# PEER expert rows 106 to 249 gathered whole instead of in halves, and the last six rows shared by TensorE and VectorE

## The chip, the cores and the metric

One core of a Trainium2 chip runs the whole kernel. The metric is the device time of one execution in microseconds, of the kernel before the median of 3 runs: 1603.6 us (1601.72 to 1604.42). Engines are named as in the profile: PE (TensorE), DVE (VectorE), ACT (ScalarE), POOL (GpSimd), SP (SyncE).

## What is computed

One decoder layer on 256 tokens of width 2048 in float32: a projection, a convolution group and a sparse attention group, an output projection and a layer norm, which give x1; then the PEER experts and a second layer norm. The change lies in the PEER part, which takes from about 430 us to the end:

```python
def peer(x, w_q, sub_keys, u_tab, v_tab):
    xt = x.reshape(n_tok, D)                                  # 256 tokens, D = 2048
    q = (xt @ w_q).reshape(n_tok, PEER_HEADS, 2, PEER_DKEY // 2)
    s = jnp.einsum('nhcd,hckd->nhck', q, sub_keys)
    s1, i1 = lax.top_k(s[:, :, 0], 16); s2, i2 = lax.top_k(s[:, :, 1], 16)
    ...                                                       # the 16 best sums of a head, of 256
    experts = jnp.take_along_axis(cand_i, pos, axis=-1)       # 8 heads x 16 experts of 16384, per token
    gates = jax.nn.softmax(top_s, axis=-1)
    h = jax.nn.gelu(jnp.einsum('td,thed->the', xb, u_tab[experts]))
    return jnp.einsum('the,thed->td', gates * h, v_tab[experts])
# then x = layer_norm(ALPHA * x1 + y, ln2_g, ln2_b)
```

## The kernel before

The 256 tokens are two tiles of 128 (tile 0, tile 1), a token per partition. A *row* s = 0 to 255 is one slot of one tile: tile s // 128, head and rank from s % 128. For a row each token needs its own expert: 2048 floats of U and 2048 of V, which lie side by side in `uv_tab` (16 KB an expert). POOL fetches them with an indirect DMA (`gather`, L512 to L515), 128 pieces, one per partition, into one of seven places of 16 KB a partition (`row[k]`, k = PLACE[s]; six places for the first 36 rows). Experts whose first key is among the 24 most frequent ones are not fetched: their number is set out of bounds, and a dense part (`dense_part`, 24 blocks of U in rows 27 to 104; `v_dense`, 24 blocks of V in rows 166 to 239; each 1 MB by SP's queue) computes them for all tokens.

What a row goes through, in this order on the engines:
- DVE `dot(s)` (L1837 to L1846, in the profile L1845): U times x1, summed, after the landing (`u_in`).
- ACT `gelu(s)` (L1271 to L1302): GELU of the dot (L1275), times the gate (`weight`, L1287 or L1289), then, up to row 247, two scalings of V by it (L1302), once V is in.
- PE `add_turned(s)` (L879 to L888): 16 products that turn V by 128 x 128 blocks and add it in PSUM, four banks a tile. From row 166 on (ADDED) it leaves out the last bank's 4, and DVE's `add_last(s)` (L1848 to L1856) adds that quarter of V in SBUF, behind the next row's dot. It is called the small addition here.
- The end of tile 1 is in token order: after row TOKEN_AT - 1 = 247 ACT copies the four banks out, PE turns them back (`turn_back(1, ...)`, L904 to L918), and rows 248 to 253 are added by PE with a diagonal of weights (`add_row`, L890 to L902, L897), four banks each. Rows 254 and 255 (TAIL = 2) are split: banks 0 and 1 by PE, banks 2 and 3 by DVE in PSUM (L2011, the bank additions), after `wait_ge(y_done, ...)`. Then the layer norm of tile 1.

Rows 0 to 25 are gathered whole, one DMA for U and V. From SPLIT = 26 up to row 253 a row is two gathers of 8 KB pieces: the U half in partition order (`u_id`), the V half with the upper and the lower 64 partitions exchanged (`v_id`), which the weights (two writes of 64 partitions, L1287) and the identity `ident_turned` (its tile is called popular in the profile) undo. POOL's order is U(s), V(s - 1), U(s + 1), ... The U half waits for the dot of the row that had the place before (`dots_done`), the V half for PE's products of that row and, for ADDED rows, its small addition (`place_read`, L517). A whole gather waits for the latter two.

DVE does other work between the dots. Up to row 105, in steps of PACE = 7 rows, it ranks the next head's keys; `gates_out` (L1820) of the head before stands behind the dot of a row with s % 7 = 0 and waits for ACT's exponentials, which ACT makes after its work on row s - 1. In rows 107 to 160 come `chunk_keys`, `chunk_gates` and `chunk_mix` for the dense gates, in rows 243 to 252 statistics, `centre` and `scale` of tile 0's layer norm.

The order on each engine is written out by hand in these loops; semaphores alone tie the engines together.

Of the kernel before, what the change touches and what calls it, by code (L numbers as in the profile page):

```python
# [56 lines left out]
TAIL = 2  # L57
TAIL_BANKS = 2
TOKEN_AT = ALL - 8
# [49 lines left out]
SPLIT_USES = [sum(SPLIT <= r and PLACE[r] == PLACE[s] for r in range(s + 1)) for s in range(ALL)]  # L109
# [3 lines left out]
def layer(nc, xT, x_tok, w_stream, w_kw, w_sub, conv_p, cln, bucket1h, rel_bias,  # L113
          b_out, ln1_col, ln_rows, uv_tab, dense_u, out):
    with ExitStack() as ctx:
# [191 lines left out]
        def weight_of(s):  # L307

            n = s if s < SPLIT else SPLIT + s - (ALL - TAIL)
            return weight[:, n:n + 1]  # L310

        def split(s):

            return SPLIT <= s < ALL - TAIL

# [67 lines left out]
        v_in = [sem(f"v_in{k}") for k in range(TAIL)]  # L383
# [4 lines left out]
        passed = {e: sem(f"passed_{e}") for e in ("pe", "act", "dve", "pool")}  # L388
# [63 lines left out]
        def _(pool):  # L452
# [70 lines left out]
            halves = uv_tab.rearrange("n (a d) -> (n a) d", a=2)  # L523
            def v_half(s):

                k, c = PLACE[s], split_col(s)
                place_read(s)
                gather(row[k][:, D:2 * D], halves, v_id[:, c:c + 1], v_half_in[k])

            for s in range(ALL):  # L530
                k = PLACE[s]
                i, j = ROW_OF[s]
                if s == 0:
                    pool.wait_ge(first_picked, 1)
# [12 lines left out]
                if s == WIDER_AT:  # L547
                    pool.wait_ge(unit_scored, LATER)
                if split(s):
                    c = split_col(s)  # L550
                    pool.wait_ge(dots_done, BEFORE_IT[s] + 1)
                    gather(row[k][:, 0:D], halves, u_id[:, c:c + 1], u_in[k])
                    if s > SPLIT:
                        v_half(s - 1)
                    if s == ALL - TAIL - 1:
                        v_half(s)
                    continue
                if BEFORE_IT[s] >= 0:
                    place_read(s)
                if s < ALL - TAIL:  # L560
                    gather(row[k], uv_tab, eid[:, i * SLOTS + j:i * SLOTS + j + 1], u_in[k])
                else:
                    j = s - (ALL - TAIL)
                    gather(row[k][:, 0:D], halves, last_id[:, 0, j:j + 1], u_in[k])
            for j in range(TAIL):
                gather(row[PLACE[ALL - TAIL + j]][:, D:2 * D], halves, last_id[:, 1, j:j + 1], v_in[j])
# [3 lines left out]
        def _(pe):  # L570
# [333 lines left out]
            def turn_back(i, banks):  # L904

                for n in banks:
# [8 lines left out]
                    if i == 1 and n == 3:  # L915
                        pe.wait_ge(y_last_done, len(ADDED))
                        last = pe.matmul(bank(1, 3), ident_turned[:, :], y_last[:, :], start=False, stop=True, skip_group_check=True)
# [100 lines left out]
            for s in range(ALL - TAIL):  # L1018
# [6 lines left out]
                if 2 <= s < TOKEN_AT:  # L1025
                    add_turned(s)
                elif s >= TOKEN_AT:
                    if s == TOKEN_AT:
                        turn_back(1, range(4))
                    add_row(s)  # L1030
# [20 lines left out]
                if BACK_AT <= s < BACK_AT + 2:  # L1051
                    turn_back(0, range(2 * (s - BACK_AT), 2 * (s - BACK_AT) + 2))
            for j in range(TAIL):
                pe.wait_ge(v_in[j], 16)
                add_row(ALL - TAIL + j, TAIL_BANKS)
# [3 lines left out]
        def _(act):  # L1059
# [6 lines left out]
            def upper(u, k):  # L1066

                act.wait_ge(w_in[k], (u - k) * (16 // RING) + 16)
                if not isinstance(u, int) or u >= RING:

                    act.wait_ge(w_used, u - (RING - 1))
                    if not isinstance(u, int):
                        act.sem_inc(passed["act"], 1)
# [317 lines left out]
        def _(dve):  # L1391
# [456 lines left out]
            def add_last(s):  # L1848

                k, n, c = PLACE[s], ADDED.index(s), split_col(s)  # L1850
                dve.wait_ge(weight_done, s + 1)
                dve.wait_ge(v_half_in[k], v_half_from[k] + 16 * SPLIT_USES[s])
                if n:
                    dve.wait_ge(y_last_done, n)
                dve.scalar_tensor_tensor(out=y_last[:, :], in0=row[k][:, D + 3 * 512:2 * D], scalar=weight_turned[:, c:c + 1],
# [7 lines left out]
            def turn_ids(c, n, ready):  # L1863

                cols, ids = slice(c, c + n), posf[1]
                dve.tensor_scalar(u_id[:, cols], ids[:, 0:n], 2.0, None, ALU.mult)
# [63 lines left out]
            for s in range(ALL - TAIL):  # L1930
# [10 lines left out]
                if t == 0 and 1 <= r - 1 < TI * PH:  # L1941
# [39 lines left out]
                if s == CHOSEN_AT + 2:  # L1981
# [11 lines left out]
                for n in range(4):  # L1993
# [3 lines left out]
                    if s == OUT_AT + 2 + n:  # L1997
                        centre(0, n)
                    if s == OUT_AT + 6 + n:
# [4 lines left out]
            for s in range(ALL - TAIL, ALL):  # L2004
                dot(s)
            dve.wait_ge(y_done, ALL - TAIL)
            for s in range(ALL - TAIL, ALL):
                dve.wait_ge(weight_done, s + 1)
                dve.wait_ge(v_in[s - (ALL - TAIL)], 16)
# [3 lines left out]
                link(last)  # L2013
            for n in range(TAIL_BANKS, 4):
# [76 lines left out]
```

## Time and profile before

| | before |
|---|---|
| median of 3 runs | 1603.6 us |
| profiled execution | 1602.62 us |
| its span | 1600.8 us |
| mean granted clock | 0.962 |

```profile
PE 1456.6 (91%) x10102; PEld 1322.7 (83%) x10102; DVE 1269.8 (79%) x2183; ACT 959.7 (60%) x1638; POOL 811.0 (51%) x521
...
PE   9999999999999989998989988888789889878886
...
DVE  5699999775777698888899989888777667657697
ACT  5433345643355557867787788677576546545582
POOL 0000110100123237766666668888888867646883
PEclk9999999999999999999999999788798999999988
DMA  7575544376599999999999999999999999999996
GB/s 258 177 249 183 199 165 158 133 267 246 201 428 424 427 423 417 416 410 405 379 396 412 407 366 344 322 353 368 352 387 394 417 417 412 414 414 405 398 352 219
```

The first line is the busy time of each engine over the span; the others cut the span into 40 slices of 40 us, a digit being the busy share in tenths. PEclk is the granted TensorE clock in tenths of 2.4 GHz, DMA the mean busy share of the 16 DMA engines, GB/s what they moved. A mean over the span says little, since the stages differ: the PEER part begins at the eleventh slice.

### The profile page before, as it was taken

What the parts mean: (1) busy time and instruction counts of PE and PEld (TensorE: products, weight loads), DVE (VectorE), ACT (ScalarE), POOL (GpSimd) and SP (SyncE); (2) the same over time, 40 slices, a digit from 0 to 9 for tenths busy, and PEclk for the clock granted to TensorE, in tenths of its full rate; (3) what the DMA queues carried; (4) which work ended last, traced back from release to release, by engine and by line L of the source; (5) the groups of instructions that cost most, each with busy time, mean ns of one, the idle gap of its engine ahead of it and who ended that gap; (6) DMA issues with size and microseconds to landing.
All of it is one profiled execution on the core that took longest, in us unless ns stands there. A gap on an engine that the chain in (4) does not pass through costs nothing.

```text
span 1600.8 us, 26707 instructions
## 1 busy us (share of the span) xinstructions
PE 1456.6 (91%) x10102; PEld 1322.7 (83%) x10102; DVE 1269.8 (79%) x2183; ACT 959.7 (60%) x1638; POOL 811.0 (51%) x521
## 2 busy tenths in 40 slices
PE   9999999999999989998989988888789889878886
PEld 8999899978889877877778877888778889878873
DVE  5699999775777698888899989888777667657697
ACT  5433345643355557867787788677576546545582
POOL 0000110100123237766666668888888867646883
PEclk9999999999999999999999999788798999999988
DMA  7575544376599999999999999999999999999996
GB/s 258 177 249 183 199 165 158 133 267 246 201 428 424 427 423 417 416 410 405 379 396 412 407 366 344 322 353 368 352 387 394 417 417 412 414 414 405 398 352 219
DMA packets 93840, 540.81 MB, mean 338 GB/s; under 512 B 28754, under 2 KB 29426, under 8 KB 32498
## 3 DMA queue, kind: packets, MB, share of 16 engines
q0 software_dynamic: 72160, 401.97, 63.6%
q1 hardware_dynamic: 20884, 137.00, 22.5%
q8 instruction: 76, 1.25, 0.3%
q14 instruction: 48, 0.39, 0.1%
q10 hardware_dynamic: 672, 0.21, 0.1%
HBM read 682.45 MB, written 4.19 MB: 429 GB/s over the span
## 4 chain that ended last, share of the span: by engine, by line
DMA 24%; DVE 17%; PE 6%; issue 6%; ACT 5%; POOL 4%; POOLq 0%; DVEq 0%; ACTq 0%
DMA uv_row<-in_uv_tab,turned 24%; DVE uv_row L1845 10%; POOL uv_row L514 4%; PE psum L886 3%; ACT uv_row L1302 3%; PE psum L897 1%; PE psum L1002 1%; ACT L1269 1%; PE psum L989 1%; DVE scratch L1675 0%; DVE first_key L1879 0%; ACT turned L1287 0%; DVE key_of L1759 0%; DVE idx L1681 0%; DVE idx L1674 0%
## 5 line engine op out<-in xcount | busy, mean ns | idle before, releaser
L514 POOL DMA_INDIRECT uv_row<-in_uv_tab,turned x456 | 729.8, 1600 | 273.6 <-issue 121.1
L1845 DVE CUSTOM_DVE_ANT_0 uv_row<-uv_row,x 128x2048 f32<-128x2048 f32 x256 | 586.9, 2293 | 142.2 <-DMA uv_row<-in_uv_tab,turned 106.3
L1302 ACT ACTIVATE uv_row<-uv_row,turned 128x1024 f32<-128x1024 f32 (+1 forms) x444 | 451.1, 1063 | 220.8 <-DMA uv_row<-in_uv_tab,turned 216.5
L886 PE MATMUL psum<-popular,uv_row 128*128 128x128 f32 x3224 | 435.8, 289 | 117.7 <-ACT uv_row L1302 116.8
L886 PEld LDWEIGHTS psum<-popular,uv_row 128*128 128x128 f32 x3224 | 380.2, 148 | 163.6 <-ACT uv_row L1302 155.7
L1002 PE MATMUL psum<-scratch,dense_unit 128*128 128x128 f32 x1536 | 188.7, 280 | 0.0
L577 PE MATMUL psum<-xT_hi,w_hi 128*128 128x256 f32 x640 | 182.9, 286 | 2.2 <-DVE w_lo L1423 2.1
L1002 PEld LDWEIGHTS psum<-scratch,dense_unit 128*128 128x128 f32 x1536 | 182.8, 197 | 0.0
L578 PE MATMUL psum<-xT_lo,w_hi 128*128 128x256 f32 x640 | 181.1, 283 | 0.0
L579 PE MATMUL psum<-xT_hi,w_lo 128*128 128x256 f32 x640 | 181.0, 283 | 0.0
L960 PE MATMUL psum<-x1T,dense_unit 128*128 128x256 f32 x768 | 180.1, 381 | 0.0
L1074 ACT ACTIVATE w_hi<-w_raw 128x2048 fp32r<-128x2048 f32 x62 | 118.8, 1916 | 85.1 <-DMA w_raw<-in_w_stream 85.1
L1423 DVE TENSOR_TENSOR w_lo<-w_raw,w_hi 128x2048 fp32r<-128x2048 f32 x62 | 141.6, 2286 | 28.6 <-ACT w_hi L1074 27.8
L960 PEld LDWEIGHTS psum<-x1T,dense_unit 128*128 128x128 f32 x768 | 141.1, 192 | 16.2
L1287 ACT ACTIVATE turned<-dots,row_gate 64x1 f32<-64x1 f32 x456 | 133.3, 292 | 11.0
L577 PEld LDWEIGHTS psum<-xT_hi,w_hi 128*128 128x128 f32 x640 | 122.7, 192 | 6.0 <-issue 2.8
L578 PEld LDWEIGHTS psum<-xT_lo,w_hi 128*128 128x128 f32 x640 | 122.7, 192 | 0.1
L579 PEld LDWEIGHTS psum<-xT_hi,w_lo 128*128 128x128 f32 x640 | 122.7, 192 | 0.0
L1275 ACT ACTIVATE dots<-dots 128x1 f32<-128x1 f32 x256 | 49.4, 193 | 84.8 <-DVE dots L1845 84.3
L514 POOL DMA_INDIRECT uv_row<-in_uv_tab,eid x26 | 38.7, 1490 | 98.2 <-PE psum L886 81.0
L1495 DVE SCALAR_TENSOR_TENSOR scratch<-glu_sb,conv_sb,scratch 128x256 f32<-128x256 f32 x203 | 82.6, 473 | 0.0
L487 POOL TENSOR_TENSOR scratch<-scratch,convT 128x256 f32<-128x256 f32 x6 | 16.5, 2745 | 130.3 <-DVE convT L1499 130.3
(287 smaller groups left out, 1778.0 us busy)
## 6 DMA issues: line engine op xcount, KB each, us to landing
w_raw<-in_w_stream SPq DMA_DIRECT2D x63, 1024.0 KB, 4.9
dense_unit<-in_dense_u SPq DMA_DIRECT2D x24, 1024.0 KB
dense_unit<-in_uv_tab SPq DMA_DIRECT2D x24, 1024.0 KB
wq_first<-in_w_stream SPq DMA_DIRECT2D x8, 1024.0 KB, 12.1
uv_row<-in_uv_tab,turned POOLq DMA_INDIRECT x456
wq_third<-in_w_stream SPq DMA_DIRECT2D x4, 1024.0 KB
xT_raw<-in_xT SPq DMA_DIRECT2D x4, 512.0 KB, 6.4
turned_rows<-dist_row POOLq DMA_DIRECT2D x1, 2048.0 KB
```

The costliest lines, as they stand in the source:

```text
L514: pool.indirect_dma_start(dst, None, tab, bass.IndirectOffsetOnAxis(ap=ids, axis=0), bounds_check=tab.shape[0] - 1, oob_is_err=False).then ...
L577: pe.matmul(dst, a[0], b[0], start=first, stop=False)
L578: pe.matmul(dst, a[0], b[1], start=False, stop=False)
L579: return pe.matmul(dst, a[1], b[0], start=False, stop=last)
L886: last = pe.matmul(bank(i, b // 4)[:, b % 4 * P:(b % 4 + 1) * P], row[k][:, D + b * P:D + (b + 1) * P], order[:, :], is_transpose=True, st ...
L960: last = pe.matmul(side[v % 2][:, 0:S], w[:, c, :], x1T[:, c, :], start=c == 0, stop=c == KC - 1)
L1002: last = pe.matmul(bank(i, n)[:, b % 4 * P:(b % 4 + 1) * P], dense_unit[v % 2][:, b * P:(b + 1) * P], mixed[:, v, i * P:(i + 1) * P], star ...
L1074: act.activation(w_hi[k], w_raw[k], ACT.Copy).then_inc(hi_done, 1)
L1287: whole = act.activation(weight_turned[to, c:c + 1], dots[of, s:s + 1], ACT.Identity, scale=row_gate[of, i, j:j + 1])
L1302: act.activation(v, v, ACT.Identity, scale=w).then_inc(scaled, 1)
L1423: dve.tensor_tensor(w_lo[k], w_raw[k], w_hi[k].bitcast(F32), ALU.subtract).then_inc(lo_dve, 1)
L1845: dve.tensor_tensor_reduce(row[k][:, 0:D], row[k][:, 0:D], x1[:, ROW_OF[s][0], :], 1.0, 0.0, ALU.mult, ALU.add, dots[:, s:s + 1]).then_inc ...
```

## The change

It does the following.
- Rows 106 to 249 (WHOLE) are gathered whole, one DMA of 16 KB pieces, in partition order. They wait for the place as a whole gather does. Their weight is one write of 128 partitions (L1289), PE turns them with `ident`, and no engine waits for a V half.
- TOKEN_AT goes from 248 to 250 and TAIL from 2 to 6: rows 248 and 249 become turned rows with a small addition, rows 250 to 255 are all shared, banks 0 and 1 by PE and 2 and 3 by DVE. All six are gathered in halves in partition order.
- DVE waits for all of `turn_back` after the dot of 251, and from then on alternates a dot and the two bank additions of the row two before.
- `gates_out` and the marking of head (0, 2) come one row later, `centre` and `scale` of tile 0 are drawn together into rows 245 to 248.
- Smaller: the row numbers in `u_id` are no longer doubled for whole rows (one more 0.17 us instruction in two of the blocks of 16 rows), the y_last product uses `ident`, unused semaphores go.

```diff
@@ -54,9 +54,9 @@
-TAIL = 2
+TAIL = 6
 TAIL_BANKS = 2
-TOKEN_AT = ALL - 8
+TOKEN_AT = ALL - TAIL
@@ -106,7 +106,16 @@
-SPLIT_USES = [sum(SPLIT <= r and PLACE[r] == PLACE[s] for r in range(s + 1)) for s in range(ALL)]
+
+WHOLE = range(IDS_AT + 1, TOKEN_AT)
+
+
+def in_two(s):
+
+    return s >= SPLIT and s not in WHOLE
+
+
+SPLIT_USES = [sum(in_two(r) and PLACE[r] == PLACE[s] for r in range(s + 1)) for s in range(ALL)]
@@ -306,12 +315,18 @@
         def weight_of(s):
 
-            n = s if s < SPLIT else SPLIT + s - (ALL - TAIL)
+            if s in WHOLE:
+                return weight_turned[:, s - SPLIT:s - SPLIT + 1]
+            n = s if s < SPLIT else SPLIT + s - TOKEN_AT
             return weight[:, n:n + 1]
 
         def split(s):
 
-            return SPLIT <= s < ALL - TAIL
+            return in_two(s) and s < TOKEN_AT
+
+        def wait_v_half(engine, s):
+
+            engine.wait_ge(v_half_in[PLACE[s]], v_half_from[PLACE[s]] + 16 * SPLIT_USES[s])
@@ -521,11 +535,16 @@
+            def in_halves(s):
+
+                return split(s) or TOKEN_AT <= s < ALL
+
             def v_half(s):
 
-                k, c = PLACE[s], split_col(s)
+                k = PLACE[s]
                 place_read(s)
-                gather(row[k][:, D:2 * D], halves, v_id[:, c:c + 1], v_half_in[k])
+                j, c = s - TOKEN_AT, split_col(s)
+                gather(row[k][:, D:2 * D], halves, last_id[:, 1, j:j + 1] if j >= 0 else v_id[:, c:c + 1], v_half_in[k])
@@ -550,20 +569,18 @@
                     pool.wait_ge(dots_done, BEFORE_IT[s] + 1)
                     gather(row[k][:, 0:D], halves, u_id[:, c:c + 1], u_in[k])
-                    if s > SPLIT:
-                        v_half(s - 1)
-                    if s == ALL - TAIL - 1:
-                        v_half(s)
-                    continue
-                if BEFORE_IT[s] >= 0:
-                    place_read(s)
-                if s < ALL - TAIL:
-                    gather(row[k], uv_tab, eid[:, i * SLOTS + j:i * SLOTS + j + 1], u_in[k])
+                elif s >= ALL - TAIL:
+                    pool.wait_ge(dots_done, BEFORE_IT[s] + 1)
+                    gather(row[k][:, 0:D], halves, last_id[:, 0, s - TOKEN_AT:s - TOKEN_AT + 1], u_in[k])
                 else:
-                    j = s - (ALL - TAIL)
-                    gather(row[k][:, 0:D], halves, last_id[:, 0, j:j + 1], u_in[k])
-            for j in range(TAIL):
-                gather(row[PLACE[ALL - TAIL + j]][:, D:2 * D], halves, last_id[:, 1, j:j + 1], v_in[j])
+                    if BEFORE_IT[s] >= 0:
+                        place_read(s)
+                    of = eid[:, s:s + 1] if s < SPLIT else u_id[:, s - SPLIT:s - SPLIT + 1]
+                    gather(row[k], uv_tab, of, u_in[k])
+                if in_halves(s) and in_halves(s - 1):
+                    v_half(s - 1)
+                if in_halves(s) and not in_halves(s + 1):
+                    v_half(s)
@@ -1024,10 +1041,6 @@
                 if 2 <= s < TOKEN_AT:
                     add_turned(s)
-                elif s >= TOKEN_AT:
-                    if s == TOKEN_AT:
-                        turn_back(1, range(4))
-                    add_row(s)
@@ -1050,8 +1063,9 @@
+            turn_back(1, range(4))
             for j in range(TAIL):
-                pe.wait_ge(v_in[j], 16)
+                wait_v_half(pe, TOKEN_AT + j)
                 add_row(ALL - TAIL + j, TAIL_BANKS)
@@ -1847,12 +1861,11 @@
             def add_last(s):
 
-                k, n, c = PLACE[s], ADDED.index(s), split_col(s)
+                k, n = PLACE[s], ADDED.index(s)
                 dve.wait_ge(weight_done, s + 1)
-                dve.wait_ge(v_half_in[k], v_half_from[k] + 16 * SPLIT_USES[s])
                 if n:
                     dve.wait_ge(y_last_done, n)
@@ -1938,7 +1954,7 @@
-                if t == 0 and 1 <= r - 1 < TI * PH:
+                if t == 1 and 1 <= r - 1 < TI * PH:
                     gates_out(r - 1)
@@ -1978,7 +1994,7 @@
-                if s == CHOSEN_AT + 2:
+                if s == CHOSEN_AT + 3:
                     mark(0, 2)
                     divide(0, 2)
@@ -1994,23 +2010,31 @@
-                    if s == OUT_AT + 2 + n:
+                    if s == OUT_AT + 2 + n // 2:
                         centre(0, n)
-                    if s == OUT_AT + 6 + n:
+                    if s == OUT_AT + 4 + n // 2:
                         scale(0, n)
@@ -1994,23 +2010,31 @@
-            for s in range(ALL - TAIL, ALL):
-                dot(s)
-            dve.wait_ge(y_done, ALL - TAIL)
-            for s in range(ALL - TAIL, ALL):
+            def add_token(s):
+
                 dve.wait_ge(weight_done, s + 1)
-                dve.wait_ge(v_in[s - (ALL - TAIL)], 16)
+                wait_v_half(dve, s)
                 for n in range(TAIL_BANKS, 4):
                     last = dve.scalar_tensor_tensor(out=bank(1, n), in0=row[PLACE[s]][:, D + n * 512:D + (n + 1) * 512],
                                                     scalar=weight_of(s), in1=bank(1, n), op0=ALU.mult, op1=ALU.add)
                 link(last)
+
+            dot(TOKEN_AT)
+            add_last(TOKEN_AT - 1)
+            dot(TOKEN_AT + 1)
+            dve.wait_ge(back_turned, 4 * TI)
+            for s in range(TOKEN_AT + 2, ALL):
+                dot(s)
+                add_token(s - 2)
+            for s in range(ALL - 2, ALL):
+                add_token(s)
```

## Rows read from the trace of the kernel before

**Rows 1.** Busy by stage: stretch, length, engines, PEclk, DMA share, GB/s.

```profile
440.00:590.00 150.00, 142.62 (x865) 128.27 (x864) 112.26 (x281) 83.34 (x137) 43.52 (x29) 0.98 1.01 426
600.00:760.00 160.00, 144.81 (x920) 127.86 (x919) 137.22 (x327) 120.86 (x206) 108.49 (x73) 0.98 1.01 412
760.00:955.00 195.00, 176.56 (x1143) 156.56 (x1141) 171.99 (x410) 152.40 (x252) 125.92 (x88) 1.00 0.99 393
955.00:998.00 43.00, 35.86 (x299) 32.58 (x298) 40.11 (x40) 37.36 (x67) 36.02 (x17) 1.00 0.93 349
998.00:1177.00 179.00, 152.50 (x1081) 144.79 (x1081) 147.53 (x148) 121.33 (x211) 153.97 (x82) 0.84 0.95 351
1177.00:1235.00 58.00, 54.82 (x363) 45.60 (x364) 38.65 (x37) 42.77 (x82) 48.61 (x31) 0.88 0.99 389
1235.00:1530.00 295.00, 255.36 (x2192) 248.51 (x2191) 200.21 (x202) 162.54 (x332) 209.90 (x138) 0.98 1.01 410
1530.00:1578.00 48.00, 39.41 (x217) 29.11 (x217) 42.88 (x48) 34.07 (x76) 41.07 (x22) 0.89 0.97 348
```

**Rows 2.** Groups of instructions, 998:1177: line, shapes, count, busy and mean, idle and releasers.

```profile
L514 POOL DMA_INDIRECT uv_row<-in_uv_tab,turned x82 | 154.0, 1878 | 25.0 <-issue 22.3 <-PE psum L886 2.7
...
L886 PE MATMUL psum<-popular,uv_row 128*128 128x128 f32 x657 | 104.3, 319 | 26.5 <-ACT uv_row L1302 26.4
```

**Rows 3.** Chain that ended last, 1050:1100 and 1380:1450: start, us, what.

```profile
1054.60 7.71 DMA uv_row<-in_uv_tab,turned
...
1358.17 24.67 DMA uv_row<-in_uv_tab,turned
...
1393.52 31.11 DMA uv_row<-in_uv_tab,turned
...
1424.64 1.60 DVE uv_row L1845
...
1428.11 28.68 DMA uv_row<-in_uv_tab,turned
```

**Rows 4.** Timeline at 1060 us: start, us, instruction, idle before it.

```profile
1059.24 0.99 POOL L514 DMA_INDIRECT uv_row<-in_uv_tab,turned  x1 [0.30 <-issue]
...
1060.45 2.29 DVE L1845 CUSTOM_DVE_ANT_0 uv_row<-uv_row,x 128x2048 f32<-128x2048 f32 x1 [2.52 <-DMA uv_row<-in_uv_tab,turned]
...
1060.54 3.07 POOL L514 DMA_INDIRECT uv_row<-in_uv_tab,turned  x1 [0.30 <-issue]
```

**Rows 5.** Waits of DVE, 760:955: for whom, us in total, times, longest.

```profile
DVE gsum L1825 <- ACT gate L1269: 15.8, 7, 2.6
```

**Rows 6.** Groups of instructions on POOL, 440:590, gathers of whole rows.

```profile
L514 POOL DMA_INDIRECT uv_row<-in_uv_tab,eid x22 | 34.7, 1576 | 93.7 <-PE psum L886 81.0 <-DVE x L1635 8.6 <-issue 4.0
```

**Rows 7.** Timeline of DVE, 984:1006, two dots three rows apart.

```profile
984.02 2.28 DVE L1845 CUSTOM_DVE_ANT_0 uv_row<-uv_row,x 128x2048 f32<-128x2048 f32 x1
...
994.83 2.28 DVE L1845 CUSTOM_DVE_ANT_0 uv_row<-uv_row,x 128x2048 f32<-128x2048 f32 x1
```

**Rows 8.** Groups of instructions on DVE, 1235:1530, the small addition.

```profile
L1855 DVE SCALAR_TENSOR_TENSOR y_last<-uv_row,turned,y_last 128x512 f32<-128x512 f32 x67 | 50.2, 749 | 20.2 <-issue 20.2
```

**Rows 9.** Timeline of the end, 1540 to 1590 us.

```profile
1540.74 2.29 DVE L1845 CUSTOM_DVE_ANT_0 uv_row<-uv_row,x 128x2048 f32<-128x2048 f32 x1
...
1552.70 2.29 DVE L1845 CUSTOM_DVE_ANT_0 uv_row<-uv_row,x 128x2048 f32<-128x2048 f32 x1
...
1563.73 1.02 PE L917 MATMUL psum<-y_last,popular 128*128 128x512 f32 x2
...
1578.16 2.29 DVE L1845 CUSTOM_DVE_ANT_0 uv_row<-uv_row,x 128x2048 f32<-128x2048 f32 x1 [4.14 <-DMA uv_row<-in_uv_tab,last_id]
...
1581.43 2.29 DVE L1845 CUSTOM_DVE_ANT_0 uv_row<-uv_row,x 128x2048 f32<-128x2048 f32 x1 [0.97 <-DMA uv_row<-in_uv_tab,last_id]
...
1585.39 2.86 DVE L2011 SCALAR_TENSOR_TENSOR psum<-uv_row,weight,psum 128x512 f32<-128x512 f32 x4 [1.66 <-PE psum L897]
```

More of the change, by code:

```diff
@@ L382, in layer @@
         u_in = [sem(f"u_in{k}") for k in range(PLACES + 1)]
-        v_in = [sem(f"v_in{k}") for k in range(TAIL)]
         dots_done, gelu_done, scaled, y_done = (sem(n) for n in ("dots_done", "gelu_done", "scaled", "y_done"))
@@ L387, in layer @@
         total_step, conv_summed, sq_step, sq_summed = (sem(n) for n in ("total_step", "conv_summed", "sq_step", "sq_summed"))
-        passed = {e: sem(f"passed_{e}") for e in ("pe", "act", "dve", "pool")}
+        act_passed = sem("act_passed")
         block = ctx.enter_context(nc.Block())
@@ L916, in turn_back @@
                         pe.wait_ge(y_last_done, len(ADDED))
-                        last = pe.matmul(bank(1, 3), ident_turned[:, :], y_last[:, :], start=False, stop=True, skip_group_check=True)
+                        last = pe.matmul(bank(1, 3), ident[:, :], y_last[:, :], start=False, stop=True, skip_group_check=True)
                     last.then_inc(back_turned, 1)
@@ L1072, in upper @@
                     if not isinstance(u, int):
-                        act.sem_inc(passed["act"], 1)
+                        act.sem_inc(act_passed, 1)
                 act.activation(w_hi[k], w_raw[k], ACT.Copy).then_inc(hi_done, 1)
@@ L1848, in add_last @@
             def add_last(s):
-                k, n, c = PLACE[s], ADDED.index(s), split_col(s)
+                k, n = PLACE[s], ADDED.index(s)
                 dve.wait_ge(weight_done, s + 1)
-                dve.wait_ge(v_half_in[k], v_half_from[k] + 16 * SPLIT_USES[s])
                 if n:
                     dve.wait_ge(y_last_done, n)
-                dve.scalar_tensor_tensor(out=y_last[:, :], in0=row[k][:, D + 3 * 512:2 * D], scalar=weight_turned[:, c:c + 1],
+                dve.scalar_tensor_tensor(out=y_last[:, :], in0=row[k][:, D + 3 * 512:2 * D], scalar=weight_of(s),
                                          in1=y_last[:, :], op0=ALU.mult, op1=ALU.add).then_inc(y_last_done, 1)
@@ L1865, in turn_ids @@
                 cols, ids = slice(c, c + n), posf[1]
-                dve.tensor_scalar(u_id[:, cols], ids[:, 0:n], 2.0, None, ALU.mult)
+                for a, b, of in ((c, WHOLE[0] - SPLIT, 2.0), (WHOLE[0] - SPLIT, WHOLE[-1] + 1 - SPLIT, 1.0), (WHOLE[-1] + 1 - SPLIT, c + n, 2.0)):
+                    a, b = max(a, c), min(b, c + n)
+                    if a < b:
+                        dve.tensor_scalar(u_id[:, a:b], ids[:, a - c:b - c], of, None, ALU.mult)
                 dve.tensor_scalar(v_id[HALF:P, cols], ids[0:HALF, 0:n], 2.0, 1.0, ALU.mult, ALU.add)
```

## The prediction

> **What bounds the kernel now.** The unit is a row: one slot s of the 256, that is one gather of a U row and a V row per token, one dot (L1845), one weighted addition. I first read the busy time by stage, with granted clock, share of the DMA engines and GB/s [rows 1], the stages cut at the dots counted in order: 600 to 955 us are rows 29 to 105, 955 to 998 rows 107 to 117, 998 to 1177 rows 118 to 159, 1177 to 1235 rows 160 to 173, 1235 to 1530 rows 174 to 241, then the end. The change touches rows 106 to 255.
>
> In 600:760, 760:955 and 1235:1530 the DMA share is 0.99 to 1.01 at 393 to 412 GB/s: the transfers bind, or nearly do. Between them, 998:1177 moves 351 GB/s. There POOL is busy 154.0 us and stands idle 25.0 us before its gathers, in pieces that are the issue of the next one, 0.3 us each [rows 2]. The sum is the whole 179: POOL never waits for a place, it is the bound. The same sum gives 48.61 + 31 x 0.3 = 57.9 of 58 us in 1177:1235, and 41.07 + 22 x 0.3 = 47.7 of 48 in 1530:1578 [rows 1]. The chain of waits says the same from the other side: a gather in it takes 7.71 us from issue to landing at 1055 us, and 31.11 us at 1393 us [rows 3]. In the one place the queue is short of work, in the other it is as full as the ring of seven places lets it be.
>
> Why a gather costs POOL 1878 ns on average [rows 2]: one takes 0.99 us, the next, issued while a dot runs, takes 3.07 us and ends at 1063.61, 0.87 us after that dot [rows 4]. Two a row cost 2 x (1.88 + 0.30) = 4.36 us, and 179 us for 41 rows (82 gathers) is 4.37.
>
> **The change, part by part. (A) gates_out one row later (t = 0 to t = 1), through row 106.** DVE waits 15.8 us in 760:955 for the exponentials, 7 times, 2.3 us each [rows 5]. One row later a dot of 2.29 us stands between and the result is there. Next in line is the DMA: the stage carries 195 x 393 = 76.6 MB, which at the 412 GB/s of the stage before takes 186 us [rows 1]. So at most 9 us, at least 0; the earlier waits of this kind lie in stages that the DMA binds and are worth nothing. I take 6. Marking (0, 2) a row later costs nothing: its identifiers are first used at row 32.
>
> **(B) One gather for two, rows 106 to 249, where POOL binds (998 to 1235, 237 us).** POOL falls to at most 3.07 + 0.3 = 3.4 us a row. If a gather of 16 KB pieces took twice as long, 2 + 0.87 + 0.3 = 3.2 us would still fit. Whole gathers exist now, in rows 0 to 25, with a mean of 1576 ns against 1878 [rows 6], so I expect no more than that. Next: DVE needs 994.83 - 984.02 = 10.81 us for three rows while it makes the chunk keys, 3.60 a row [rows 7]; 42 rows are 151 us, a gain of at most 28. And the DMA: 351 x 179 + 389 x 58 = 85.4 MB, which is 200 us at the 426 GB/s of 440:590 (where rows are whole), 208 at 410, 213.5 at 400, 217 at 393 [rows 1]. I take 400 (reason under C): a gain of 23.5 us. Ends: 33 (151 us, and 53 for the last fourteen rows) and 10 (over half of it kept by other waits).
>
> Beside this stand ACT, which loses one of two weight writes and its wait for the V half, and PE. PE is 152.5 us busy of 179 at a mean clock of 0.84, and idle for ACT's scaled rows in the rest (26.4 us) [rows 1, 2]. In 955:998 rows went at DVE's pace with PE busy 35.86 of 43 and the clock at 2.4 GHz throughout [rows 1]. So I cost PE at nothing; what it costs without that cover is the second rival.
>
> **(C) The same where the DMA binds (1235 to 1530, 295 us, 410 GB/s, 121 MB).** For: rows that are whole move at 426 GB/s, halves at 412 and 410 [rows 1]; 121 MB would then take 284 us, 11 less. Against: a half of a place is given back early now. The U half that lands at 1424.62 is read by its dot, and the next U gather of the place is issued at 1428.11, 3.5 us later; flights are 24.67 to 31.11 us [rows 3]. A whole place comes back only when its V has been read too, last by the small addition of DVE, which stands behind the dot of the next row, and that dot waits for the next landing. A period is 295 us for 69 rows (138 gathers), 4.3 us, so this is 4.3 + 2.3 + 0.75 [rows 8] = 7.4 us, with POOL's own wait some 8. Of a place's round of 7 x 4.3 = 30 us, about 22 are then in flight. A shorter queue evens out less between the 16 engines, whose shares of kept experts differ from row to row. The nearest rows are 351 GB/s with 7.7 us in flight and 410 with 25 to 31. I take 400, between the 393 and the 410 of the busy stages: 302.5 us, a loss of 7.5. Ends: a gain of 11, and a loss of 18 (386 GB/s).
>
> The Trainium skill (HBM Reference, "Specifications (TRN2)") says that a core streaming alone reaches about 425 GB/s, bounded by its 16 DMA engines. By that figure B and C together would take 206.4 / 0.425 = 486 us, 46 less than now. The stage 440:590 agrees (426); the stages of rows with left-out experts do not reach it (412, 393, 410), and the sum goes by them.
>
> **(D) The end, from the dot of row 244 (1540.74) to the last bank addition (1588.25).** Moving the centre and scale steps of tile 0 forward changes no sum. Added on DVE: two small additions (rows 248, 249) of 0.75 us, and eight bank additions (twelve for four) of 2.86 / 4 = 0.72: 7.2 us. Gone: its waits for the last two landings, 4.14 and 0.97, and for PE, 1.66 [rows 8, 9]. The landings are late because POOL issues back to back there, which one gather a row up to 249 ends; PE is late because it multiplies 28 banks, and 12 remain. A new wait: after the dot of 251 DVE stands at back_turned (all four banks), with four dots and twelve additions queued behind it. Now the last row ahead of that turn, 247, has its dot over at 1554.99 and the turn over at 1564.75, 9.8 us [rows 9]. DVE fills 2 x 2.29 + 2 x 0.75 = 6.1 of them, 3.7 is wait. Sum: 7.2 - 6.8 + 3.7 = +4.1. Ends: 0 (the turn is sooner, since ACT has a weight less to write) and +8 (a landing is late after all).
>
> Sum: -6 - 23.5 + 7.5 + 4.1 = -17.9. The profiled execution has 1602.6 us (span 1600.8 and 1.8 around it), so 1584.7; the median of the runs is 1.0 above it, 1585.7. I write 1585.
>
> **Rivals. (1) The queue stays full with 22 us in flight.** Whole rows move at 418 GB/s in C (289.5 us), B ends at DVE's pace. A -9, B -33, C -5.5, D +2: -45, 1558. For: 426 GB/s in 440:590. Against: in those rows no expert is left out, in the later ones the engines' loads are uneven.
>
> **(2) PE keeps what POOL gives.** If the clock stays at a mean of 0.84 in 998:1177 and half of PE's 26.4 us of idle stays between ACT's scaling and its products, that stage needs 152.5 + 13 = 165.5 us and B is worth 13.5: -6 - 13.5 + 7.5 + 4.1 = -8, 1595. For: PE is busy 85% there. Against: 955:998 at full clock, with rows at 3.6 us.
>
> **(3) Slower: the ring starves the DMA.** A whole place returns only when its V has been read, and some engines run dry while others hold the row up. B and C carry 206.4 MB in 532 us. With A and D (-6 + 4) the change breaks even at 534 us, a mean rate of 386 GB/s; below that it loses. At 369, halfway from 386 to the 351 of the short queue, it is 559 us: +25, 1627. For: 348 to 351 GB/s in every stage where little is in flight [rows 1]. Against: 22 us is nearer to the full queue than to 7.7.
>
> The Trainium skill (DMA: Bandwidth & Descriptors, "The descriptor swizzle") has it that a 128-partition transfer gives each engine a fixed set of 8 partitions, and partitions 64 apart go to different engines. The halves, whose V side is swapped by 64, then spread a token's load over two engines, and whole rows put it on one. That speaks for this rival and against the change; no row here shows a single engine.
>
> **How the numbers follow.** Forecast 0.62 (own range 1575 to 1597), rival 1 0.14, rival 2 0.14, rival 3 0.10. The range, 1563 to 1600, leaves out rival 3 and the better half of rival 1. A measurement tells about 0.2% (3.2 us) from no change: faster 0.85, within 0.06, slower 0.09.
>
> **What would show it.** A: no DVE wait for the gates, and the dot of row 106 some 6 us earlier. B: POOL idle for PE or for places and not for issue between rows 118 and 159, some 3.8 us a row, about 400 GB/s. C: the rows of this stage at 4.4 us each, flights near 22 us; 410 GB/s or more speaks for rival 1, under 386 for rival 3. D: a DVE wait of 3 to 4 us ahead of the dot of 252, none for the last landings. What would make it wrong: whole rows outside 393 to 410 GB/s, or a whole gather that holds POOL longer than a half does.

## The result and the profile after

The median of 22 runs is 1605.8 us, against 1600.1 us for 22 runs of the kernel before on the same chips: a ratio of 1.0038, 95% interval 1.0026 to 1.0050. The change makes the kernel slower by 0.4%. The prediction said 1585 and gave 0.09 to slower. The profiled execution has 1606.4 us, its span 1604.5 (before 1602.6 and 1600.8).

The page of after, in the order of the lines shown of before: busy time over the span, then slices of 40 us.

```profile
PE 1446.6 (90%) x10094; PEld 1321.9 (82%) x10094; DVE 1274.6 (79%) x2195; ACT 929.8 (58%) x1492; POOL 568.6 (35%) x377
...
PEclk9999999999999999999999998897899999999978
DMA  7565544376599999999999999999999999999993
GB/s 258 180 243 182 198 168 158 132 299 225 225 426 426 425 422 416 417 411 408 380 403 416 405 365 380 366 420 382 354 381 421 405 349 407 418 388 365 359 364 133
```

POOL has 144 gathers less and is busy 568.6 us in place of 811.0. In the six slices from 960 us on the rate is 354 to 420 GB/s where it was 322 to 387, but in the three from 1400 us on it is 359 to 388 where it was 398 to 414. By stage, the cuts at the same dots as in [rows 1] (rows 106, 118, 160, 174, 241), in its columns:

```profile
600.00:760.00 160.00, 145.57 (x906) 127.24 (x905) 138.63 (x327) 120.53 (x204) 108.47 (x73) 0.97 1.01 413
760.00:947.00 187.00, 176.29 (x1129) 157.17 (x1128) 167.93 (x399) 148.09 (x250) 125.88 (x80) 0.98 0.99 393
947.00:997.00 50.00, 40.85 (x306) 38.07 (x304) 41.22 (x45) 35.15 (x57) 19.72 (x13) 0.90 0.96 383
997.00:1170.00 173.00, 147.14 (x1105) 140.09 (x1104) 147.25 (x148) 115.19 (x173) 63.19 (x43) 0.88 0.95 382
1170.00:1222.00 52.00, 49.56 (x369) 43.04 (x370) 37.97 (x37) 37.46 (x64) 29.28 (x13) 0.97 0.98 393
1222.00:1530.00 308.00, 259.02 (x2170) 252.38 (x2168) 196.49 (x200) 150.38 (x267) 96.98 (x67) 0.96 0.96 386
```

The dots of after that cut the stages, from the timeline of DVE (start, us, instruction, idle before it): rows 106, 118, 160, 174 and 241.

```profile
946.63 2.29 DVE L1859 CUSTOM_DVE_ANT_0 uv_row<-uv_row,x 128x2048 f32<-128x2048 f32 x1 [1.96 <-DMA uv_row<-in_uv_tab,turned]
...
997.33 2.29 DVE L1859 CUSTOM_DVE_ANT_0 uv_row<-uv_row,x 128x2048 f32<-128x2048 f32 x1
...
1170.39 2.29 DVE L1859 CUSTOM_DVE_ANT_0 uv_row<-uv_row,x 128x2048 f32<-128x2048 f32 x1 [1.68 <-DMA uv_row<-in_uv_tab,turned]
...
1222.35 2.29 DVE L1859 CUSTOM_DVE_ANT_0 uv_row<-uv_row,x 128x2048 f32<-128x2048 f32 x1
...
1531.77 2.29 DVE L1859 CUSTOM_DVE_ANT_0 uv_row<-uv_row,x 128x2048 f32<-128x2048 f32 x1
```

| dots of rows | before | after | difference |
|---|---|---|---|
| up to 106 | 954.7 | 946.6 | -8.1 |
| 106 to 118 | 43.5 | 50.7 | +7.2 |
| 118 to 174 | 236.8 | 225.0 | -11.8 |
| 174 to 241 | 294.8 | 309.4 | +14.6 |

The 8.1 us before row 106 are given back by row 118, and the 11.8 of the rows up to 174 are given back, and 2.8 more, by row 241. Rows 241 to 244 take 0.9 us less and the end 2.3 more (below), which adds up to +3.3; the spans differ by 3.7. In 947:997 rows no longer go at DVE's pace: the dot of row 106 waits 1.96 us for its landing, at 383 GB/s.

In 997:1170 POOL is no longer the bound. The groups of instructions of that stage, with the idle time before them:

```profile
L903 PE MATMUL psum<-ident,uv_row 128*128 128x128 f32 x672 | 100.3, 307 | 24.7 <-ACT uv_row L1316 24.5
L1859 DVE CUSTOM_DVE_ANT_0 uv_row<-uv_row,x 128x2048 f32<-128x2048 f32 x42 | 96.2, 2291 | 21.3 <-DMA uv_row<-in_uv_tab,turned 21.0
...
L528 POOL DMA_INDIRECT uv_row<-in_uv_tab,turned x43 | 63.4, 1474 | 111.3 <-PE psum L903 108.6 <-issue 2.7
```

Where POOL had only issue time ahead of its gathers [rows 2], it waits 108.6 us for PE's products, that is for a place to come back, and a gather costs 1474 ns, not 1878. DVE's dots wait 21.0 us for landings, about as long as before (21.6 us in 998:1177). The chain of waits of after, 1000:1170 and then 1380:1450, has these flights (start, us):

```profile
1030.76 16.06 DMA uv_row<-in_uv_tab,turned
...
1123.70 25.41 DMA uv_row<-in_uv_tab,turned
...
1356.04 26.00 DMA uv_row<-in_uv_tab,turned
...
1393.38 27.29 DMA uv_row<-in_uv_tab,turned
...
1424.51 27.99 DMA uv_row<-in_uv_tab,turned
```

The chain picks out gathers that ended a wait. Over all gathers issued in a stage the median from issue to landing is 20.5 us in 997:1170 and 23.7 us in 1235:1530 (the number of gathers, the median):

```profile
uv_row<-in_uv_tab,turned POOLq DMA_INDIRECT x43, 20.5
uv_row<-in_uv_tab,turned POOLq DMA_INDIRECT x64, 23.7
```

The queue had run down to 7.7 us before row 160 [rows 3]; now it is full, and yet it moves 382 GB/s in the one stage and 386 in the other. The question for the experiments is why a queue so full moves so little.

### The profile page after: what moved, and what is told of

It reads as the page before. It is cut to its first block, busy times and chain, and to the rows that moved or that the text cites. A ratio compares the mean times of both kernels' runs of the same rounds, so it can differ in the third digit from the quotient of the medians.

```text
span 1604.5 us, 26126 instructions
## 1 busy us (share of the span) xinstructions
PE 1446.6 (90%) x10094; PEld 1321.9 (82%) x10094; DVE 1274.6 (79%) x2195; ACT 929.8 (58%) x1492; POOL 568.6 (35%) x377
## 4 chain that ended last, share of the span: by engine, by line
DMA 38%; PE 33%; DVE 17%; issue 6%; ACT 4%; POOL 2%; SPq 0%; POOLq 0%; DVEq 0%; ACTq 0%
DMA uv_row<-in_uv_tab,turned 33%; PE psum L903 9%; PE psum L594 4%; DVE scratch L1509 4%; PE psum L595 4%; PE psum L596 4%; DVE uv_row L1859 4%; DMA uv_row<-in_uv_tab,eid 3%; DVE w_lo L1437 3%; PE psum L945 3%; PE psum L977 3%; ACT uv_row L1316 2%; PE psum L1019 2%; POOL uv_row L528 2%; PE psum L1006 1%
## 5 line engine op out<-in xcount | busy, mean ns | idle before, releaser
L528 POOL DMA_INDIRECT uv_row<-in_uv_tab,turned x304 | 471.1, 1550 | 508.1 <-PE psum L903 261.4
L1316 ACT ACTIVATE uv_row<-uv_row,turned 128x1024 f32<-128x1024 f32 x448 | 454.7, 1062 | 47.3 <-DMA uv_row<-in_uv_tab,turned 40.8
L903 PE MATMUL psum<-ident,uv_row 128*128 128x128 f32 x2384 | 331.4, 294 | 99.6 <-ACT uv_row L1316 98.7
L903 PEld LDWEIGHTS psum<-ident,uv_row 128*128 128x128 f32 x2384 | 290.8, 152 | 126.2 <-ACT uv_row L1316 123.0
L1289 ACT ACTIVATE dots<-dots 128x1 f32<-128x1 f32 x256 | 51.1, 200 | 295.2 <-DVE dots L1859 294.9
L903 PE MATMUL psum<-popular,uv_row 128*128 128x128 f32 x1280 | 163.7, 280 | 26.8 <-ACT uv_row L1316 26.3
L903 PEld LDWEIGHTS psum<-popular,uv_row 128*128 128x128 f32 x1280 | 145.8, 144 | 48.1 <-ACT uv_row L1316 43.0
L977 PEld LDWEIGHTS psum<-x1T,dense_unit 128*128 128x128 f32 x768 | 143.2, 195 | 16.9
## 6 DMA issues: line engine op xcount, KB each, us to landing
turned_rows<-dist_row POOLq DMA_DIRECT2D x1, 2048.0 KB, 14.3
```

Source lines behind the costliest of these rows:

```text
L528: pool.indirect_dma_start(dst, None, tab, bass.IndirectOffsetOnAxis(ap=ids, axis=0), bounds_check=tab.shape[0] - 1, oob_is_err=False).then ...
L903: last = pe.matmul(bank(i, b // 4)[:, b % 4 * P:(b % 4 + 1) * P], row[k][:, D + b * P:D + (b + 1) * P], order[:, :], is_transpose=True, st ...
L977: last = pe.matmul(side[v % 2][:, 0:S], w[:, c, :], x1T[:, c, :], start=c == 0, stop=c == KC - 1)
L1316: act.activation(v, v, ACT.Identity, scale=w).then_inc(scaled, 1)
```

## The experiments

Ratios are to the kernel before, run beside each kernel on the same chip; its medians there lie between 1599.8 and 1600.7 us. A difference between the medians of two experiments is known to 3 to 5 us either way. Two theories at the start. *Engines:* a token's U and V pieces now go through the same DMA engine, so that an engine whose tokens keep many experts in a row is the last by twice as much. *Ring:* a whole place comes back later, and too little is queued.

### One suspected cause at a time, in the kernel before

**e1: the V half in partition order.** Halves, gathers, waits and instruction counts stay; only the exchange by 64 goes, in the row numbers (below), the weights' two writes and the identities.

```diff
-                dve.tensor_scalar(v_id[HALF:P, cols], ids[0:HALF, 0:n], 2.0, 1.0, ALU.mult, ALU.add)
-                dve.tensor_scalar(v_id[0:HALF, cols], ids[HALF:P, 0:n], 2.0, 1.0, ALU.mult, ALU.add).then_inc(turn_ready, 1)
+                dve.tensor_scalar(v_id[HALF:P, cols], ids[HALF:P, 0:n], 2.0, 1.0, ALU.mult, ALU.add)
+                dve.tensor_scalar(v_id[0:HALF, cols], ids[0:HALF, 0:n], 2.0, 1.0, ALU.mult, ALU.add).then_inc(turn_ready, 1)
...
-                order = ident_turned if split(s) else ident
+                order = ident
```

> The kernel before, with the V half gathered in partition order instead of with its 64-partition halves exchanged; the count of instructions, their sizes and all waits stay. If the loss of whole rows comes from U and V of a token lying on the same DMA engine (theory 1, uneven engines), this alone is slower than before: by 10 to 20 us, 1610 to 1620, with the GB/s of rows 174 to 241 down from 410 to about 395. If it comes from the place that is given back late (theory 2, the ring), nothing changes: 1600, within 3.

Measured: 1635.6 us, ratio 1.0237 (1.0209 to 1.0266), 35 us slower, about twice what was expected of this theory. Busy by stage of this kernel (columns as in [rows 1]):

```profile
600.00:760.00 160.00, 139.68 (x875) 120.89 (x874) 131.79 (x312) 116.19 (x198) 98.72 (x70) 0.98 0.99 399
998.00:1177.00 179.00, 158.53 (x1131) 152.37 (x1132) 150.35 (x150) 125.68 (x219) 153.71 (x84) 0.83 0.94 351
1235.00:1510.00 275.00, 229.62 (x1956) 223.73 (x1955) 176.92 (x178) 144.43 (x296) 193.39 (x126) 0.98 1.00 398
```

Where POOL binds (998:1177) nothing changes, 351 GB/s; where the DMA binds the rate falls from 412 to 399 and, in 1235:1510, from 412 to 398. The order of the V pieces alone costs 3% of the rate there (6% in 760:955, 370 for 393), and it holds for rows 26 to 247, a longer stretch than that of the change. From the dot of row 174 to that of row 241 this kernel takes 311.6 us, 16.9 more than before and as long as the changed kernel (309.4). Six kernels with exchanged halves there (before, e3, e7, e8, e11, e12) took 295 to 302 us in their traces.

**e2: the U half held back.** It waits for the whole place, as a whole gather does; order as before.

```diff
-                    pool.wait_ge(dots_done, BEFORE_IT[s] + 1)
+                    place_read(s)
```

> The kernel before, with the U half of rows 26 to 253 waiting for the same as a whole gather does: that PE and DVE have read the V of the row that had the place. Two gathers a row and the exchanged halves stay. Theory 2 (the ring): flights of the U half fall from about 30 to 24 us between 1380 and 1450, and the kernel is 8 to 15 us slower, 1608 to 1615. Theory 1 (uneven engines): within 3 us of before, since POOL issues as often and the engines' loads are as even as before.

Measured: 1610.1 us, ratio 1.0085 (1.0056 to 1.0114), 10 us slower; 405 GB/s in 600:760, and 368 in 998:1177, where POOL binds. The shorter ring costs too, though less than the order. It is shorter here than in the changed kernel: over rows 174 to 241 the next U gather of a place is issued 12.8 us after the dot of the row that had it, on average, against 7.1 before and 8.9 for the whole gathers of after.

### The parts of the change

**e3: the changed kernel with no whole rows** (parts A and D remain; the identity and the row numbers follow).

```diff
-WHOLE = range(IDS_AT + 1, TOKEN_AT)
+WHOLE = range(TOKEN_AT, TOKEN_AT)
```

> The changed kernel with no whole rows beyond 25: rows 26 to 249 are halves as before, but the new order at the end (six shared rows) and the moved gates_out stay. This is the change without its main part. If the end costs the 3 to 4 us that the two traces show and the gates are worth nothing, it takes 1602 to 1604, and whole rows are worth -2 to +4. If the whole rows lose what the change loses, it takes 1598 to 1600. If the end is all of the loss, 1606.

Measured: 1598.3 us in 12 runs, ratio 1.0002 (0.9981 to 1.0024). So the whole rows cost 1605.8 - 1598.3 = 7.5 us (by the two ratios, 0.0036, it is 5.8). Forecast was B and C together, -16.

**e4: the changed kernel with gates_out and the marking back where they were.**

```diff
-                if t == 1 and 1 <= r - 1 < TI * PH:
+                if t == 0 and 1 <= r - 1 < TI * PH:
```

> The changed kernel with gates_out and the marking of (0, 2) where they were. My forecast gave the move 6 us: then this takes 1612. The two traces show the dot of row 106 8.1 us earlier but the landing of its U 1.6 us later, so the move only uses up the lead of the DMA: then this takes 1604 to 1608, no difference from the changed kernel.

Measured: 1612.3 us, ratio 1.0079 (1.0049 to 1.0108): A is worth 6.5 us in the changed kernel.

**e11: the kernel before with A alone**, the reverse edit.

> The kernel before with gates_out and the marking of (0, 2) one row later and nothing else: part A alone. My step A said 6 us, and putting it back in the changed kernel cost 6.5: 1594, against 1600.3. The changed kernel with halves alone (A and D) took 1598.3, so D is worth +4 if this takes 1594. If A is worth nothing without whole rows: 1600.

Measured: 1595.4 us in 12 runs, ratio 0.9977 (0.9954 to 1.0000), 4.5 us faster. Between this kernel and e3 lies D alone: 1598.3 - 1595.4 = 2.9 us slower, which is not clear of the noise by itself.

**e7: whole rows only up to 165**, where the V block products of the dense part begin; halves behind.

```diff
-WHOLE = range(IDS_AT + 1, TOKEN_AT)
+WHOLE = range(IDS_AT + 1, VALUES_AT)
```

> The changed kernel with whole rows from 106 to 165 only, where POOL binds, and halves with exchanged partitions from 166 to 249. Both theories: it keeps the 11 us that the landing of row 174 came earlier and does not pay the 11 us after it. 1588 to 1592, against 1598.3 of the changed kernel with halves alone and 1605.8 of the changed kernel. If the gain is lost anyway because the later stage starts with a more uneven queue: 1598.

Measured: 1591.5 us, ratio 0.9946 (0.9924 to 0.9968). Against e3, whole rows 106 to 165 are worth 6.8 us; against the changed kernel, whole rows 166 to 249 cost 14.3.

### Even engines: the two causes taken away

The theory of the engines rests on the left-out experts being unevenly spread. These kernels leave out other experts than the reference, by a fixed pattern in place of the 24 most frequent keys: in every row 5 or 6 of 8 pieces are kept in every group of eight partitions (0 to 3 with 32 to 35, and so on), equally in the lower and the upper 64, about as many bytes as before (406.4 MB through POOL's queue against 402.0).

```diff
-                link(dve.scalar_tensor_tensor(out=posf[1][:, 0:n], in0=of, scalar=float(SKIP), in1=ids, op0=ALU.mult, op1=ALU.add))
+                link(dve.scalar_tensor_tensor(out=posf[1][:, 0:n], in0=even_out[:, j:TOP], scalar=float(SKIP), in1=ids, op0=ALU.mult, op1=ALU.add))
...
+def _even():
+
+    p, r = np.arange(P)[:, None], np.arange(TOP)[None, :]
+    eighth = (p & 3) + 4 * ((p >> 5) & 1)
+    return ((eighth + 3 * r) % 8 < 2 + (r % 3 == 0)).astype(np.float32)
```

**e5 and e6: the kernel before and the changed kernel with this edit.**

> The kernel before with another choice of which experts are not fetched: by a fixed pattern of token and rank, so that each group of eight partitions (0 to 3 and 32 to 35, and so on) fetches 5 or 6 experts in every row, 70.3% of all, instead of those whose first key is frequent (71.1% by the count of the packets). It leaves out and adds experts that the reference has otherwise, so it computes something else with the same instructions. Theory 1 (uneven engines): the DMA-bound stages run at 415 GB/s or more, while POOL still binds between rows 118 and 173: 1575 to 1590. Theory 2 (the ring alone): no change but for 1% fewer bytes, 1594 to 1600.

> The same fixed pattern in the changed kernel. Theory 1: with the engines even, whole rows bring what the prediction wanted of B and C: 25 to 30 us less than the kernel before with this pattern, so 1548 to 1562, at 420 GB/s or more in rows 118 to 241. If the place that comes back late is the greater part of the loss, whole rows still do not win: within 5 us of the kernel before with this pattern.

Measured: before 1592.1 us (ratio 0.9942, 0.9921 to 0.9963), after 1547.7 (0.9672, 0.9640 to 0.9703). The first lies between the ranges of the two theories, its rate of 416 GB/s in that of the first. With the even pattern the change is worth 44 us: 41.4 of them lie between the dots of rows 118 and 174 (239.2 to 197.8 us), and 6.5 between those of 174 and 241 (292.0 to 285.6). Busy by stage, first of e5, then of e6:

```profile
998.00:1177.00 179.00, 147.56 (x1086) 139.72 (x1086) 144.80 (x145) 121.59 (x211) 153.69 (x84) 0.88 0.93 343
1235.00:1510.00 275.00, 239.49 (x2056) 231.90 (x2054) 187.07 (x188) 151.25 (x310) 177.10 (x130) 0.99 1.02 416
```

```profile
998.00:1177.00 179.00, 164.27 (x1307) 147.76 (x1306) 168.30 (x168) 141.04 (x217) 91.93 (x51) 0.98 1.00 417
1235.00:1510.00 275.00, 229.09 (x1965) 221.12 (x1964) 201.02 (x210) 151.68 (x268) 124.97 (x71) 0.99 1.01 423
```

These two kernels carry the same experts through the same ring of places. The one with whole rows moves 417 and 423 GB/s where the real pattern gave it 381 and 386. In 998:1177 DVE is busy 168.3 of 179 us: rows go at DVE's pace, PE at a granted clock of 0.98.

**e9: e5 with the V half in partition order** (the edit of e1).

> Both V in partition order and the fixed even pattern, in the kernel before: the control for theory 1. If unevenness of the engines is the whole of the 35 us that V in partition order cost, the order makes no difference here: 1592, within 4, as the kernel before with this pattern. If something else in that order costs (the writes into one group of partitions, the weights), it stays slower: 1610 or more. The output isn't the reference's, since other experts are left out.

Measured: 1589.9 us, ratio 0.9919 (0.9890 to 0.9949), 2 us below e5, within the noise. The same edit costs 35 us with the real pattern. So it isn't the order in itself (the products, the identity, the address pattern): the order costs only where the left-out experts are unevenly spread over the partitions.

**e10: e5 with the U half held back** (the edit of e2).

> The U half held until the place's V has been read, with the fixed even pattern: the ring alone, without uneven engines. With uneven engines holding it cost 10 us. If a late place costs only because a shorter queue evens out less, it costs at most 3 us here: 1590 to 1595. If it costs by itself: 1600 or more. The output isn't the reference's, since other experts are left out.

Measured: 1593.0 us, ratio 0.9954 (0.9933 to 0.9975), 1 us above e5, against 10 with the real pattern; 416 GB/s in 1235:1510 in both. A ring that is shorter by this much costs only with the uneven pattern.

**Landings in the traces.** Each gather raises its semaphore sixteen times, and the traces hold the times of these steps, with a few missing. For the U halves and whole rows of 174 to 241, the last step came after the middle one by this much on average:

| | real pattern, us | even pattern, us |
|---|---|---|
| halves, V exchanged | 9.2 (before), 9.8 (e11) | 3.0 (e5) |
| halves, V in partition order | 12.5 (e1) | 2.0 (e9) |
| whole rows | 12.6 (after) | 4.2 (e6) |

In rows 118 to 160 of after the sixteen steps of a gather spread over 13.0 us from first to last, and over 6.1 us in e6. So a gather waits for a late part of itself, and the part is later with the real pattern, most of all where U and V of a token go the same way. Which DMA engine a step belongs to isn't recorded.

### A version between the two

**e8: every second row whole, from 107 to 165**, the rest halves with the exchanged V. POOL is relieved by a quarter of its gathers there, and half of the rows keep their V on other engines.

```diff
-WHOLE = range(IDS_AT + 1, TOKEN_AT)
+WHOLE = range(107, 166, 2)
```

> As whole rows 106 to 165, but only every second row there (107, 109, ... 165) is whole; the others are exchanged halves. POOL issues three gathers for two rows, 1.5 x (1.88 + 0.3) = 3.3 us a row, just under DVE's 3.6, and only half of the rows put a token's U and V on one engine. Theory 1: as good as whole rows 106 to 165 or up to 5 us better, 1584 to 1592. If the count of POOL's gathers is all that matters: 3 to 8 us worse than whole rows 106 to 165.

Measured: 1584.1 us, ratio 0.9885 (0.9847 to 0.9923), 7.4 us below e7, which has the same end.

**e12: the same rows and A, but the end as it was before** (TAIL = 2, TOKEN_AT = 248).

> Every second row from 107 to 165 whole, gates_out one row later, and the end as in the kernel before (two shared rows, the turn after row 247). Against 1584.1 with the new end this measures D in the fastest kernel so far: if D costs the 4 us of the sum, 1580. If the new end is worth something once the rows before it are earlier, 1586 or more.

Measured: 1578.2 us, ratio 0.9849 (0.9817 to 0.9880): the fastest of all with the real pattern, 21.6 us under the kernel before. D costs 1584.1 - 1578.2 = 5.9 us here. Its stages, and POOL's gathers in 998:1177:

```profile
998.00:1177.00 179.00, 155.16 (x1198) 144.11 (x1197) 157.49 (x157) 135.59 (x219) 131.96 (x72) 0.92 0.99 393
1235.00:1510.00 275.00, 232.93 (x2002) 227.16 (x2001) 183.31 (x186) 150.22 (x307) 199.68 (x128) 0.98 1.01 406
```

```profile
L525 POOL DMA_INDIRECT uv_row<-in_uv_tab,turned x72 | 135.7, 1885 | 47.3 <-PE psum L898 24.4 <-issue 17.4 <-DVE dots L1857 5.6
```

POOL is no longer the bound (30.0 of its 47.3 idle us are waits for PE and DVE, 17.4 issue), the DMA share is 0.99 at 393 GB/s, and the last stage keeps 406.

## Why the prediction was wrong, point by point

**What bounds the kernel: right.** POOL bound 998:1177, and with fewer gathers it was free: 108.6 us of waits for places in 997:1170 against 22.3 of issue before. In the seven kernels of the experiments that have halves there (e1, e2, e3, e5, e9, e10, e11) POOL stays 152 to 154 us busy in 998:1177 and the stage moves 343 to 368 GB/s.

**(A), -6: right in size by the runs, in part by another path.** One wait of 2.5 us for the gates remains of seven, where none was forecast:

```profile
DVE gsum L1839 <- ACT gate L1283: 2.5, 1, 2.5
```

The DMA was next, as forecast: the queue's lead ahead of row 106 is used up (the wait of 1.96 us at 946.63). e4 gives 6.5 and e11 4.5. What the sum left out is the stage behind it, rows 106 to 117, which it took to go on at DVE's pace (43 us). They took 50.7, and did so in e3 too, with halves (945.6 to 996.7, 51.0 us): so most of what A shows at row 106 is only drawn forward. The dot of row 118 starts at 998.2 before, at 997.3 in after and at 991.3 in e11. By the runs the net of A is near the forecast 6; in which rows it is gained isn't shown.

**(B), -23.5: the right mechanism, the wrong rate.** This is the first term that failed, and the larger one. "I take 400" set the DMA's rate for rows 118 to 173; measured were 382 and 393 GB/s in the stages 997:1170 and 1170:1222 of after, and the stretch gained 11.8 us in place of 23.5. By the runs, whole rows 106 to 165 are worth 6.8 us. Of the two ends, the working had "10 (over half of it kept by other waits)": the landings were that wait. The traces with halves took 229 to 239 us for these rows, so the 11.8 of one pair of traces is known to some 5 us only.

**(C), +7.5: the right sign, half the size, and mostly for another reason.** The rate was 386, the lower end of the sum (+18); rows 174 to 241 took 14.6 us more, and e7 against the changed kernel has 14.3 for rows 166 to 249. The ring was sized about right: the forecast had about 22 us of a place's round in flight, and the median flight is 23.7 us, in a round of 7 x 309.4 / 67 = 32 us. What the forecast took too good was the ring of the kernel before, read from a single gather of the chain: over rows 174 to 241 the next U gather of a place was issued 7.1 us after the dot on average, not 3.5. So a place came back only 2 us later (8.9 for 7.1), and the queue was nearly as full as before. The step that failed is again "I take 400, between the 393 and the 410 of the busy stages". The working names the uneven engines, but lets them cost only through a shorter queue; that U and V of a token now land the same way was given no price. e1 shows that price without any whole row: +16.9 us in the same rows. The nearest rows taken, 393 to 410 GB/s, were all of halves with the exchanged V; no row of before shows a late whole row, and 426 GB/s in 440:590 was of whole rows without left-out experts.

B and C together: forecast -16, measured +7.5 (after against e3, about 3 us either way). Split by e7, the rows up to 165 gave 6.8 us where some 23 were forecast, and those behind cost 14.3 where 7.5 were. In all the forecast was -17.9 and the measurement +5.7: the error of 23.6 us is that of B and C. The base of the forecast, 1603.6 us from 3 runs, was 3.5 us above the 1600.1 of 22 runs.

**(D), +4.1: right in sign and about in size.** The forecast wait ahead of the dot of 252 is there, 2.1 us for 3.7:

```profile
1574.15 2.29 DVE L1859 CUSTOM_DVE_ANT_0 uv_row<-uv_row,x 128x2048 f32<-128x2048 f32 x1 [2.11 <-PE psum L934]
...
1576.36 1.41 DVE L2025 SCALAR_TENSOR_TENSOR psum<-uv_row,weight,psum 128x512 f32<-128x512 f32 x2
...
1587.35 4.31 DVE L2025 SCALAR_TENSOR_TENSOR psum<-uv_row,weight,psum 128x512 f32<-128x512 f32 x6
```

The waits of 4.14 and 0.97 for the last landings [rows 9] are gone; behind the turn a dot and two additions alternate without a gap. From the dot of 244 (1541.85) to the end of the last addition it is 49.8 us for 47.5. The runs give +2.9 (e3 against e11) and +5.9 (e8 against e12), each known to 4 to 5 us.

**The rivals.** Rival 3 had the sign and the point: whole rows lose below a mean of 386 GB/s, and the stages of B and C ran at 382, 393 and 386. Its price of +25 supposed 369. At 382 to 393 GB/s, around its break-even, the loss was 5.7 us. Of its two mechanisms, "some engines run dry while others hold the row up" is what the runs bear out, by e1 (+35 us) against e9 (-2) and e2 (+10) against e10 (+1). "The ring starves the DMA" alone is refuted by e10. Rival 1 (the queue stays full, -45) is what happens with the even pattern: e6 against e5 has -44, at 417 and 423 GB/s. Rival 2 isn't what held the rows in the main: PE's clock rose to 0.88 and 0.97 in the two stages, DVE waited for landings and not for PE. Places do come back through PE's products, but these are 17.1% of the chain in 1000:1170, and landings 73.0%.

The Trainium skill (DMA: Bandwidth & Descriptors, "The descriptor swizzle") says of a transfer to 128 partitions that each engine writes a fixed set of 8 of them, with partitions 64 apart on different engines. The runs agree as far as they can: pairing U with the V of the partition 64 away saves 35 us (e1), and nothing measurable when the load is even by those sets (e9). The prediction set this rule against the change but gave the rival 0.10; nothing in the rows of before spoke against the rule itself, only the flights were thought to cover it.

What stays open: no row shows a single engine's load, so that it is the imbalance between engines is inferred from the crossing of e1, e2, e9 and e10 and from the steps of the landings. The even pattern also makes the rows nearly equal among each other in bytes, and how much of the 44 us is due to that wasn't separated; the 35 us of e1 are free of this, since its rows carry the same bytes as before. That the changed kernel would have kept its gain with the V side exchanged inside one 16 KB piece can't be tried, since one piece has one partition.

## What to carry to other kernels

When a gather skips pieces, bytes over a mean rate do not give its time: here the same bytes took 35 us longer in another order (e1). Before merging two transfers, ask which of their pieces then go the same way, and keep two transfers of one token apart where loads are uneven. Merge only so many gathers as the issuing engine needs: with the same end, every second row from 107 to 165 took 1584 us (e8), all of 106 to 165 1591 (e7), all of 106 to 249 1606. A rate taken from rows of another kind (no piece left out, or another order) is no bound for the sum.

## What the hardware showed that was not expected

- The same bytes in the same number of gathers took 35 us longer (1600 to 1636 us) when U and V of a token had the same partition. A DMA share near 1.00 does not say that the rate can't rise: 1.00 went with 398 GB/s (e1), 1.01 with 410 (before) and with 423 (e6).
- With even engines the gathers of 8 KB pieces reached 416 GB/s and those of 16 KB pieces 423, with the real pattern 412 and 386 in the same stage (1235:1510). The larger pieces are not slow by their size: e1, with 8 KB pieces and U and V in the same partition, lost as much in rows 174 to 241.
- A whole gather holds POOL no longer than a half: 1474 ns on average in 997:1170, where a half took 1878 before, and the two here took 0.99 and 2.75 us.

```profile
1060.86 0.99 POOL L528 DMA_INDIRECT uv_row<-in_uv_tab,turned  x1 [2.58 <-PE psum L903]
...
1069.30 2.75 POOL L528 DMA_INDIRECT uv_row<-in_uv_tab,turned  x1 [2.72 <-PE psum L903]
```
